# Down products of an expert layer in rounds of 512 columns: two token groups share four column groups

## The reference

```python
probs = jax.nn.softmax(logits, axis=-1)
top_p, top_e = lax.top_k(probs, TOP_K)              # 2 of 8 experts
top_p = top_p / jnp.sum(top_p, axis=-1, keepdims=True)
...
def swiglu(h, w_gate, w_up, w_down):                # (n, 1024) -> (n, 3584) -> (n, 1024)
    return (jax.nn.silu(h @ w_gate) * (h @ w_up)) @ w_down
...
out = jnp.zeros((T + 1, d), jnp.float32).at[slot_tok].add(ys.astype(jnp.float32) * slot_p[:, None])
```

## Time and profile before

| | us |
|---|---|
| median of 3 runs | 1347.28 |
| lowest and highest | 1343.73, 1347.76 |
| span of the profiled execution | 1342.1 |
| time of the profiled execution beside its span | not given apart from the three runs |
| TensorE busy | 1285.0 |
| VectorE, ScalarE, GpSimd busy | 214.8, 125.5, 19.3 |
| bytes read from HBM | 458.94 MB |

### The profile page before, as it was taken

One profiled execution on the slowest core, in us unless ns is written; L12 is line 12 of the kernel. 1 busy time (PEld: TensorE's weight loads), 2 busy tenths in 40 slices (PEclk: granted clock), 3 DMA queues, 4 the chain that ended last, 5 costly groups with the idle time before them and its releaser, 6 DMA issues.

```text
span 1342.1 us, 28835 instructions
## 1 busy us (share of the span) xinstructions
PE 1285.0 (96%) x12945; PEld 742.3 (55%) x12946; DVE 214.8 (16%) x592; ACT 125.5 (9%) x249; POOL 19.3 (1%) x107
## 2 busy tenths in 40 slices
PE   7899999999999699999999999999999999999995
PEld 3777788877886444346543434665343555343553
DVE  0298200000004501010010201002010002010002
ACT  2201310000002310000001000001000001000002
POOL 1000000000002000000000000000000000000000
PEclk9999999999999799999999999999999999999998
DMA  9999467656536299999999899999999999999993
GB/s 336 406 403 390 165 247 243 221 167 231 175 126 242 83 408 417 418 420 424 418 404 355 342 383 422 391 375 419 417 418 420 423 418 418 419 418 419 422 420 133
DMA packets 87886, 462.25 MB, mean 344 GB/s; under 512 B 8747, under 2 KB 12119, under 8 KB 52663
## 3 DMA queue, kind: packets, MB, share of 16 engines
q1 hardware_dynamic: 85937, 456.41, 85.3%
q10 hardware_dynamic: 1814, 3.85, 0.8%
HBM read 458.94 MB, written 2.24 MB: 344 GB/s over the span
## 4 chain that ended last, share of the span: by engine, by line
PE 82%; DMA 13%; issue 2%; DVE 1%; ACT 1%; POOL 1%; SPq 0%; ACTq 0%; DVEq 0%; POOLq 0%
PE bank L1610 36%; PE bank L1364 25%; DMA ring<-in_w_exp_down_dram 13%; PE bank L1632 9%; PE bank L1333 3%; PE bank L1558 2%; PE bank L1664 1%; PE bank L1581 1%; PE bank L1321 1%; PE bank L1262 1%; PE bank L1490 1%; DMA pm_rows<-pmT 0%; PE bank L1502 0%; SPq L502 0%; DVE xT L923 0%
## 5 line engine op out<-in xcount | busy, mean ns | idle before, releaser
L1610 PE MATMUL bank<-ring,HT 128*32 128x512 f32 (+1 forms) x5376 | 510.3, 539 | 3.7 <-DMA ring<-in_w_exp_up_dram 3.4
L1610 PEld LDWEIGHTS bank<-ring,HT 128*32 128x32 f32 x5376 | 180.4, 110 | 321.7 <-issue 308.9
L1364 PE MATMUL bank<-HT,ring 128*128 128x264 f32 x1024 | 232.9, 389 | 2.5 <-POOL HT L594 2.5
L1364 PEld LDWEIGHTS bank<-HT,ring 128*128 128x128 f32 x1024 | 194.6, 191 | 44.0 <-issue 11.1
L1632 PE MATMUL bank<-ring,hid_t 128*32 128x256 f32 x2560 | 149.0, 379 | 2.7 <-DMA ring<-in_w_exp_down_dram 2.7
L1632 PEld LDWEIGHTS bank<-ring,hid_t 128*32 128x32 f32 x2560 | 85.5, 110 | 57.3 <-issue 5.2
L1364 PE MATMUL bank<-BIG,ring 128*128 128x264 f32 x480 | 108.0, 386 | 0.0
L1364 PEld LDWEIGHTS bank<-BIG,ring 128*128 128x128 f32 x480 | 91.1, 190 | 15.5
L1632 PE MATMUL bank<-ring,COND 128*32 128x256 f32 x1568 | 89.3, 380 | 8.5 <-DMA ring<-in_w_exp_down_dram 8.3
L1632 PEld LDWEIGHTS bank<-ring,COND 128*32 128x32 f32 x1568 | 50.0, 110 | 46.3 <-DMA ring<-in_w_exp_down_dram 16.1
L1199 DVE TENSOR_TENSOR hid_t<-bank,hid_t 128x512 f32<-128x512 f32 (+1 forms) x22 | 14.2, 643 | 360.1 <-PE bank L1610 359.6
(11 more groups left out here) (224 smaller groups left out, 528.7 us busy)
## 6 DMA issues: line engine op xcount, KB each, us to landing
ring<-in_w_exp_gate_dram SPq DMA_DIRECT2D x64, 1024.0 KB, 14.6
ring<-in_w_exp_up_dram SPq DMA_DIRECT2D x64, 1024.0 KB, 15.7
ring<-in_w_exp_down_dram SPq DMA_DIRECT2D x64, 1024.0 KB, 23.6
ring<-in_w_ada_dram SPq DMA_DIRECT2D x48, 1024.0 KB, 12.5
ring<-in_w_exp_gate_dram SPq DMA_DIRECT2D x64, 768.0 KB, 15.6
ring<-in_w_exp_up_dram SPq DMA_DIRECT2D x64, 768.0 KB, 14.1
ring<-in_w_exp_down_dram SPq DMA_DIRECT2D x32, 1536.0 KB, 25.0
ring<-in_w_in_dram SPq DMA_DIRECT2D x10, 1024.0 KB, 25.5
```

The lines of the kernel that those rows point to most:

```text
L1364: ins = t_.matmul(banks_of[label][:, 0:NT], w[:, k, f * P:(f + 1) * P], src(k0 + k), start=(k0 + k == 0), stop=(k0 + k == k_tiles - 1))
L1610: ins = t_.matmul(bank[GATE_BANKS[role][g]][i * GRP:(i + 1) * GRP, 0:cols], xg[:, k, c0:c0 + GRP], w[:, i, :], start=(k == 0), stop=(k == ...
```

## The change

In `down`, two neighbouring token groups form a block. Its four column groups take: group g with columns 0 to 511 and 512 to 1023, group g + 1 with the same. Each product has 512 columns and a block fills one bank. A group left over is done as before, except that its column groups take the 256-column pieces in the order 0, 2, 1, 3. The table `BLOCKS` says which groups form blocks: large 3 as 2 + 1, large 5 as 2 + 2 + 1, small 2 as 2, small 1 as 1.

With a wide block, row groups 0 and 1 of `out_rows` hold one token group's 1024 outputs over two groups' space, and row groups 2 and 3 the other's. So the place product takes two passes for each half h. The first takes all blocks, with row groups in the order 0, 2, 1, 3 for banks 0 to 3. The second takes the wide blocks alone, with the order 2, 0, 3, 1. Since the second pass writes the banks from other row groups than the first, TensorE waits between the passes for the end of its own first pass (`placed_half`). `place` has one matrix for each block, in which partitions 0 to 63 and 64 to 127 stand for different tokens, and the slot numbers for these are made by three iotas a quarter instead of two.

```diff
+BLOCKS = {("large", 3): ((0, 2, 0), (2, 1, 2)), ("large", 5): ((0, 2, 0), (2, 2, 1), (4, 1, 3)),
+          ("small", 1): ((0, 1, 1),), ("small", 2): ((0, 2, 0),)}
+BLOCK_MOST = {"large": 3, "small": 1}
+PLACES = 4
+ROW_GROUPS = ((0, 2, 1, 3), (2, 0, 3, 1))
+FIRST_COL = {2: (0, 4 * P, 0, 4 * P), 1: (0, 4 * P, 2 * P, 6 * P)}
...
             for j in range(QUAD):
-                here, half = slot_i[j * GRP:(j + 1) * GRP, :], 2 * MOST["large"]
-                link(g.iota(here[:, 0:half], [[CAPS[0], 2], [GRP, MOST["large"]]], base=GRP, channel_multiplier=-1))
-                link(g.iota(here[:, half:2 * half], [[CAPS[1], 2], [GRP, MOST["large"]]], base=1, channel_multiplier=1))
+                here, at = slot_i[j * GRP:(j + 1) * GRP, :], GRP * (j // 2)
+                large = here[:, 0:8].rearrange("p (a b) -> p a b", a=2)
+                link(g.iota(large[:, :, 0:2], [[CAPS[0], 2], [2 * GRP, 2]], base=GRP + at, channel_multiplier=-1))
+                link(g.iota(large[:, :, 2:4], [[CAPS[0], 2], [2 * GRP, 2]], base=3 * GRP, channel_multiplier=-1))
+                link(g.iota(here[:, 8:12], [[CAPS[1], 2], [-at, 2]], base=1 + at, channel_multiplier=1))
...
-                    for g in range(n):
-                        v.scalar_tensor_tensor(place[r * MOST["large"] + g], posb[:, bass.ds(i, 1), :].rearrange("p o n -> p (o n)"),
-                                               slot_col[:, r, bass.ds(pass_now[0], 1), g:g + 1].rearrange("p a b -> p (a b)"),
+                    blocks = BLOCKS[role, n]
+                    for b, (_, _, entry) in enumerate(blocks):
+                        v.scalar_tensor_tensor(place[r * BLOCK_MOST["large"] + b], posb[:, bass.ds(i, 1), :].rearrange("p o n -> p (o n)"),
+                                               slot_col[role][:, bass.ds(pass_now[0], 1), entry:entry + 1].rearrange("p a b -> p (a b)"),
...
-                            for g in range(groups):
-                                b = bank[OUT_BANKS[role][g // 2]]
+                            for g, n_groups, _ in BLOCKS[role, groups]:
+                                b, cols = bank[OUT_BANKS[role][g // 2]], n_groups * DQ
                                 for i in range(QUAD):
-                                    ins = t_.matmul(b[i * GRP:(i + 1) * GRP, (g % 2) * DQ:(g % 2 + 1) * DQ],
-                                                    hidT[role, half][g][:, c0:c0 + GRP], w[:, jj, i * DQ:(i + 1) * DQ],
-                                                    start=bool(first and jj == 0 and g % 2 == 0),
+                                    d0 = FIRST_COL[n_groups][i]
+                                    ins = t_.matmul(b[i * GRP:(i + 1) * GRP, 0:cols],
+                                                    hidT[role, half][g + (i // 2 if n_groups == 2 else 0)][:, c0:c0 + GRP], w[:, jj, d0:d0 + cols],
+                                                    start=bool(first and jj == 0),
...
                 for h in range(2):
-                    for role in ROLES:
-                        for g in range(count[role]):
-                            if (h, role, g) == (0, "small", 0):
+                    for half, row_groups in enumerate(ROW_GROUPS):
+                        blocks = [block for block in every if block[1] == 2] if half else every
+                        if half:
+                            pe.wait_ge(on("placed_half"), p * 2 + h + 1)
+                        for at, n_groups, where in blocks:
+                            if (h, half, at) == (0, 0, L):
                                 pe.wait_ge(on("small_rows_ready"), p + 1)
...
+                            for i, r in enumerate(row_groups):
+                                c0 = (2 * i + h) * P - FIRST_COL[n_groups][r]
+                                ins = t_.matmul(bank[PLACE_BANKS[h][i]][:, 0:NT], rows[r * GRP:(r + 1) * GRP, c0:c0 + P],
+                                                where[r * GRP:(r + 1) * GRP, :], start=(not half and at == 0),
+                                                stop=bool(half and (at, n_groups) == blocks[-1][:2]))
...
+                        if not half:
+                            ins.then_inc(on("placed_half"), 1)
```

## The result

| | before | after |
|---|---|---|
| median of 5 runs, us | 1345.06 | 1352.03 |
| lowest and highest | 1343.73, 1347.76 | 1350.89, 1353.47 |
| span of the profiled execution | 1342.1 | 1350.0 |
| its own time | not given apart | 1351.86 |

The ratio is 1.0045, 95% interval 1.0029 to 1.006: the change makes the kernel slower by 0.45%, and the interval leaves out 1. The time lies inside the range given (1343.5 to 1354.0), but the likeliest case was +1.3 us, no measurable change, and the medians differ by 7.0 us.

What follows compares the result with a forecast made beforehand. DMA was taken to bound pairs 0, 2 and 3, TensorE pair 1. Slot tables +0.4, fetches -0.4, place waits +0.8 twice and wide blocks -0.3 gave +1.3 us on the 1347.28 median: 1348.6, range 1343.5 to 1354.0.

Steps and rivals of the forecast that it cites:

- rival 1: Place product: each wait between the passes costs 1.64 us, not 0.4; +6.3 us in all, 1353.6; chance 0.10.
- What bounds the kernel: Path: DMA to pair 0's end, TensorE from its place product to about 902 us, DMA to 1320 us, then tail.
- Wide blocks, -0.34 us in pair 1: Down products: 448 fewer MATMULs a pair save 0.76 ns each, counting only in pair 1.
- rival 2: Down products: a narrow instruction's fixed part is real, 41 ns for each of 448 in pair 1; about 1330; chance 0.04.
- Instructions not fetched, -0.4 us: Three DMA-bound pairs: 896 fewer instructions a pair save 55 kB of traffic, 0.13 us each.
- Place product, +0.8 us each time: Pairs 0 and 3: two new waits of TensorE between passes, 0.4 us each; those of pairs 1 and 2 are covered.
- Slot tables, +0.4 us: Program start: 12 iotas for 8 add 0.84 us, of which a wait for w_ada takes back 0.45.
- Rival 3, the turn from pair 0 to pair 1: Turn and gather before pair 1: clock and loop turn may change, -1.3 us or, in strong form, +7.0; chance 0.18.
- strong form: Rival 3's second case: pair 1's whole gather at half clock, 5.7 us more, +7.0 in all, 1355.6; chance 0.06.
- The sum: Whole kernel: +0.4 - 0.4 + 0.8 - 0.3 + 0.8 = +1.3 us, 1348.6, not measurable.
- The signs named beforehand: Wrong if pair 1 over 2 us shorter, place-product gaps over 1 us, or DMA below 415 GB/s in a narrow pair.

Runs made afterwards that it cites:

- e3: Changed kernel with the second place pass using the first pass's row-group order and no wait between the passes; 1348.48 us in one run.
- e6: Changed kernel with executed-over padding in both loop bodies, so pair 1's code begins 132 slots before a block's end, as before the change; 1346.09 us, ratio 1.0000.
- e10: Changed kernel padded so that pair 1's code begins 250 slots before a block's end; 1347.59 us in 12 runs, ratio 1.0020.
- e12: Changed kernel padded so that pair 1's code begins 152 slots before a block's end; 1344.49 us in 12 runs, ratio 0.9992.
- e13: Changed kernel with 220 dead slots in the narrow body, so pair 1's code begins 40 slots before a block's end; 1349.2 us in one run.
- e2: Kernel before, with padding meant to move pair 1's code but absent from the compiled program, so a repeat of that kernel; 1343.9 us, ratio 0.9997.
- e5: Changed kernel with the whole loop over pairs placed 128 instructions later; 1349.22 us in one run.
- e7: Kernel before with 128 dead slots in the narrow body, so pair 1's code begins 4 slots before a block's end; 1358.56 us, ratio 1.0091.
- e11: e10 with the twelve slot-table iotas and their copy moved behind the signal TensorE's first product waits for; 1348.80 us in 12 runs, ratio 1.0024.

## Why the prediction was right or wrong, step by step

The number came out inside the range, and that was luck. The step that failed is the turn from pair 0 to pair 1, which the sum had at nothing: 8.6 us more idle time of TensorE, and a gather longer by 0.8. The range held because its upper end had room for rival 1, which did not happen, and because it was laid around 1347.28 us, the median of three runs, where five have 1345.06. Laid around that, it would have ended at 1351.8, below the 1352.03 measured.

- **What bounds the kernel.** Right. The path goes over TensorE from pair 0's place product through pair 1, and it is this that made the stop expensive: 8.6 us more in the turn were 9.0 at the end of pair 1's down products and 7.9 at the end of the kernel.
- **Wide blocks, -0.34 us in pair 1.** Right: 72.66 became 72.38, -0.28 us for 448 MATMULs, 0.6 ns each. By the Trainium skill's 60 cycles (TensorEngine Tiling (Array Packing), Instruction Overhead) it would be an estimated 11 us. The measured 0.28 us is against it, and rival 2 fell.
- **Instructions not fetched, -0.4 us.** The bytes are right (0.25 MB against 4 x 55 kB). Pair 0's last load comes 198.51 us after the gather's start in place of 199.12, 0.61 us less and more than the 0.13 forecast; what the rest is I did not test. This step is also where the reasoning failed: it counted the code as bytes to be moved and not as a place from which TensorE must read in time. 3.5 blocks less in the narrow form are 0.05 MB and nearly no transfer time, but half a block decides where the next form begins.
- **Place product, +0.8 us each time.** Right: 4.70 became 5.45 us, 0.38 a wait by e3, where 0.4 was forecast. Rival 1 (1.64 us) fell. The estimate of 0.28 us from the Trainium skill (TensorE: Matmul & The Clock Gate, Single matmul latency) was below what was measured; its formula is stated for a bf16 product over the full array, and these are float32 products of 32 rows. At the kernel's end the tail is longer by 0.35 us and not 0.8, mostly because ten of the last products in the chain (line 1679, now 1698) take 1.32 us in place of 1.94.
- **Slot tables, +0.4 us.** Right at the start, and too small to be seen later. The first product is later by 0.64 us, not 0.84: the iotas are smaller now and follow each other by 0.19 us, not 0.21, so that twelve of them take 2.33 us where eight took 1.67.

```profile
4.91 0.12 POOL L579 IOTA slot_i<- 32x4 int32 x1
...
7.68 1.02 PE L1273 MATMUL bank<-ident,BIG 9*128 9x9 f32 x8 [7.68 <-POOLq L584]
```

The first big product (line 1364, now 1375) begins at 39.66 in place of 39.21, +0.45 us, but in e6, e10, e12 and e13, whose program is the same up to there, it begins at 39.11 to 39.31. The +0.26 at the gather of pair 0 is as little a measurement of this term: the same code brings that gather between 463.61 and 466.74 us.
- **Rival 3, the turn from pair 0 to pair 1.** The right place and the wrong mechanism. I wrote that "the code of the loop becomes shorter" and priced the turn by its 2.50 us and the clock; my strong form needed the whole gather at half clock. The turn itself grew by 8.6 us, to which the gather's lower clock added 0.8. The missing term of the sum is this one: at the first jump into a form of the code TensorE has to wait for its next block, and before the change 132 slots of work hid that. A part of the turn before was such a wait too (its gather begins 3.15 us after a packet's end), which is why turns could also become shorter: those after pairs 1 and 2 fell from 1.68 and 2.27 us to 0.99 and 0.96. The time of the strong form, 1355.6, has the other terms' 1.3 us twice; 1347.28 + 7.0 is 1354.3.
- **The sum.** +1.3 us was forecast and the span grew by 7.9: the turn and gather brought 9.3, the other terms 0.4 up to the place product's end and 0.35 in the tail. Given back were 0.7 in pair 1 (0.28 of it the wide blocks, the rest lies before its down products and is not settled) and 1.4 between the hole and the last load. Of that 0.26 are fetches by the forecast's reckoning, and the rest is open too. Two executions of one and the same program can differ by more than these open parts: the kernel before spans 1342.1 us here and 1339.6 in e2. With the layout put right (e6) nothing measurable is left, as the forecast, which lacked this term, had it.
- **The signs named beforehand.** "DMA below 415 GB/s in a narrow pair" was not seen (418 and 419; pair 3 has 393, as before), nor gaps over 1 us in the place product. None of the signs looked at the turn, where a stop would have stood out at once.

## What to carry to other kernels

When a change removes or adds many instructions on an engine that branches between bodies of code, count in the compiled program how many slots lie between each jump's target and the next block boundary, and between the last boundary and each jump, before and after. Here 4 slots in place of 132 cost more than all the other terms of the change together, and an alignment of the code won it back. Such a stop cost what it lasted where TensorE was the bound or the ring of loads filled up during it, and nothing where loads were behind; so look first at the jumps where the ring is full, and compare two versions of a kernel only with their code laid out alike.

## What the runs showed that I had not expected

- A block of instructions comes late. In the kernel after two packets of the instruction queue lie between 674 and 682 us, some 6 us apart, the second arrives 10 us after the place product's end, and TensorE goes on 1.3 us after that. In e3, e5 and e13 it arrives at 679.5, 681.2 and 680.6 us, and TensorE goes on 1.3 to 1.5 us later. A packet itself takes 1.1 us. The weights filled the DMA engines all that time (share 1.01), which may be why; no run has the jump without them.
- A shift of the code alone, with no other edit, is worth 0.91% of this kernel (e7).
- The stop has a cost behind it: the granted clock falls behind an idle stretch. The gather took 10.52 us at a mean of 0.75, partly at 1.2 and partly at 2.4 GHz, after a stop of 10 us. In e5 and e6, where TensorE had stood for 1.2 us, it took 8.06 us at 1.00. Between the two, the same program had 8.06 us after a turn of 2.30 (e2) and 9.74 after one of 2.54 (the kernel before).
- A start that is earlier by 2.5 us (e11) was down to 0.7 us at 38 us, behind the wait for w_ada, and gone at the gather of pair 0, with a lower clock in between.
